# A fourth pair of converted-weight buffers in the expert loop, and one transposition a unit earlier

## What is computed

```
def expert(args):
    wg, wu, wd, ix, g = args
    xe = t[ix]
    he = jax.nn.silu(xe @ wg) * (xe @ wu)
    return (he @ wd) * g[:, None].astype(he.dtype)
```

## Time and profile before

| | us |
|---|---|
| median of 3 runs | 2207.47 |
| lowest, highest run | 2193.83, 2209.68 |
| profiled execution, device time | 2186.04 |
| its span, first to last instruction | 2184.2 |
| PE busy | 2122.7 (97%) |
| DVE busy | 1570.7 (72%) |
| ACT busy | 1359.3 (62%) |
| mean DMA rate over the span | 286 GB/s |

### The profile page before, as it was taken

How to read it: one execution, slowest core, us unless ns; L and a number is a source line. 1 busy time by engine, 2 the same in 40 slices (tenths; PEclk the granted TensorE clock), 3 DMA queues, 4 the chain that set the end, 5 groups by cost and what they waited for, 6 DMA issues and landing times.

```text
span 2184.2 us, 27119 instructions
## 1 busy us (share of the span) xinstructions
PE 2122.7 (97%) x10388; PEld 1580.5 (72%) x10388; DVE 1570.7 (72%) x1203; ACT 1359.3 (62%) x1069; POOL 232.9 (11%) x138
## 2 busy tenths in 40 slices
PE   8999999999959999999999999999999999999997
PEld 6858878887846776777677777767767777777765
DVE  5384452234458887888888888888888888798885
ACT  5273362223226777777777777777777777767764
POOL 2102210000120101010110101001010101101010
PEclk9999999999979999999999999999999999999998
DMA  6202131132328999999999999999999999999994
GB/s 235 77 18 105 55 122 58 61 132 71 152 104 325 368 388 363 379 370 377 375 369 377 375 380 371 367 384 366 376 372 381 372 370 388 366 374 375 375 367 184
DMA packets 71916, 623.96 MB, mean 286 GB/s; under 512 B 8352, under 2 KB 8480, under 8 KB 19264
## 3 DMA queue, kind: packets, MB, share of 16 engines
q1 hardware_dynamic: 64128, 595.70, 70.5%
q0 software_dynamic: 7744, 27.67, 4.4%
HBM read 609.70 MB, written 13.63 MB: 285 GB/s over the span
## 4 chain that ended last, share of the span: by engine, by line
PE 84%; DVE 6%; DMA 6%; ACT 3%; issue 1%; POOL 0%; SPq 0%; ACTq 0%; DVEq 0%; POOLq 0%
PE PS L543 26%; PE PS L545 25%; PE PS L544 25%; DMA x_w_raw<-in_w_expert_gate 4%; DVE x_w_low L1187 3%; ACT x_w_high L1117 2%; PE PS L652 2%; PE PS L898 1%; PE PS L635 1%; DMA x_w_raw<-in_w_expert_up 1%; PE PS L666 1%; PE PS L552 1%; DMA w_raw<-in_w_in 1%; PE PS L842 1%; PE PS L763 0%
## 5 line engine op out<-in xcount | busy, mean ns | idle before, releaser
L1187 DVE TENSOR_TENSOR x_w_low<-x_w_raw,x_w_high 128x3072 fp32r<-128x3072 f32 x383 | 1177.9, 3087 | 234.2 <-ACT x_w_high L1117 232.1
L1117 ACT ACTIVATE x_w_high<-x_w_raw 128x3072 fp32r<-128x3072 f32 (+1 forms) x384 | 980.3, 2558 | 259.7 <-PE PS L545 197.7
L543 PE MATMUL PS<-x_w_high,xT_high 128*96 128x512 f32 (+1 forms) x1536 | 580.0, 378 | 4.9 <-DVE x_w_low L1187 4.8
L545 PE MATMUL PS<-x_w_high,xT_low 128*96 128x512 f32 (+1 forms) x1536 | 575.1, 374 | 0.0
L544 PE MATMUL PS<-x_w_low,xT_high 128*96 128x512 f32 (+1 forms) x1536 | 573.2, 373 | 0.0
L543 PEld LDWEIGHTS PS<-x_w_high,xT_high 128*96 128x96 f32 x1536 | 248.1, 162 | 98.8 <-DVE x_w_low L1187 13.3
L545 PEld LDWEIGHTS PS<-x_w_high,xT_low 128*96 128x96 f32 x1536 | 248.0, 161 | 90.1
L544 PEld LDWEIGHTS PS<-x_w_low,xT_high 128*96 128x96 f32 x1536 | 248.6, 162 | 85.7
L543 PE MATMUL PS<-x_w_high,hidden_high 128*96 128x512 f32 x704 | 281.2, 399 | 0.0
L545 PE MATMUL PS<-x_w_high,hidden_low 128*96 128x512 f32 x704 | 276.6, 393 | 0.0
L544 PE MATMUL PS<-x_w_low,hidden_high 128*96 128x512 f32 x704 | 275.8, 392 | 0.0
(11 more groups left out here) (189 smaller groups left out, 1703.3 us busy)
## 6 DMA issues: line engine op xcount, KB each, us to landing
x_w_raw<-in_w_expert_gate SPq DMA_DIRECT2D x96, 1536.0 KB, 8.5
x_w_raw<-in_w_expert_up SPq DMA_DIRECT2D x96, 1536.0 KB, 8.8
x_w_raw<-in_w_expert_down SPq DMA_DIRECT2D x96, 1536.0 KB, 8.5
x_w_raw<-in_w_expert_gate SPq DMA_DIRECT2D x32, 1024.0 KB, 7.3
x_w_raw<-in_w_expert_up SPq DMA_DIRECT2D x32, 1024.0 KB, 7.3
x_w_raw<-in_w_expert_down SPq DMA_DIRECT2D x32, 1024.0 KB, 7.1
w_raw<-in_w_in SPq DMA_DIRECT2D x19, 1024.0 KB, 4.8
x<-in_x_sample SPq DMA_DIRECT2D x8, 512.0 KB, 11.5
```

Source lines behind the costliest of these rows:

```text
L543: mm(out, sh, mh, start=first, stop=False)
L545: return mm(out, sl, mh, start=False, stop=last)
L1117: a_(xh[:, w % SPLITS, 0:n], xraw[:, w % RAWS, 0:n], ACT.Copy).then_inc(x_high, 1)
L1187: return v.tensor_tensor(out, src, high.bitcast(F32), ALU.subtract)
```

## The change

`SPLITS` goes from 3 to 4. The four pairs are no longer one array with an index but four arrays each; the fourth pair lies at columns 960 and 4032, where the residual rows were. ACT therefore converts unit 3 ahead of the loop too, behind the first two halves of tokens and behind a wait for all six residual stores, and DVE makes its low part before the loop. In the loop, step u converts unit u + 4. `tokens` 1 goes from behind unit 22 to behind unit 21, after `hidden` 5: with four pairs, the low part that stands behind `tokens` 1 in step 22 is that of unit 2 of the next expert, and in step 21 that of unit 1, which is the first that reads the second half of the tokens.

```diff
@@ -88,7 +88,7 @@
-RAWS, SPLITS = 4, 3
+RAWS, SPLITS = 4, 4
@@ -101,7 +101,7 @@
         after("up", 2, 1): [("tokens", 0)], after("down", 1, 1): [("hidden", 4)],
-        after("down", 1, 2): [("hidden", 5)], after("down", 2, 0): [("tokens", 1)]}
+        after("down", 1, 2): [("hidden", 5), ("tokens", 1)]}
@@ -194,14 +194,14 @@
-        xl = at("x_w_low", 7104, SPLITS * XUNIT, dt=F32R).rearrange("p (b n) -> p b n", b=SPLITS)
-        xh = at("x_w_high", 16320, SPLITS * XUNIT, dt=F32R).rearrange("p (b n) -> p b n", b=SPLITS)
+        xl = [at(f"x_w_low{i}", off, XUNIT, dt=F32R) for i, off in enumerate((7104, 10176, 13248, 960))]
+        xh = [at(f"x_w_high{i}", off, XUNIT, dt=F32R) for i, off in enumerate((16320, 19392, 22464, 4032))]
...
-        xraw = at("x_w_raw", 31680, RAWS * XUNIT).rearrange("p (b n) -> p b n", b=RAWS)
+        xraw = [at(f"x_w_raw{i}", off, XUNIT) for i, off in enumerate((31680, 34752, 37824, 40896))]
...
@@ -1114,13 +1114,13 @@
                 n = unit_width(w)
-                a_(xh[:, w % SPLITS, 0:n], xraw[:, w % RAWS, 0:n], ACT.Copy).then_inc(x_high, 1)
+                a_(xh[w % SPLITS][:, 0:n], xraw[w % RAWS][:, 0:n], ACT.Copy).then_inc(x_high, 1)
...
-            for w in range(1, SPLITS):
+            for w in range(1, 3):
                 unit_high(0, w)
@@ -1136,6 +1136,8 @@
             for q in range(PRE):
                 misc_high("tokens", q, q + 1, 6 + q)
+            act.wait_ge(S("x", "residual_stored"), 16 * NT)
+            unit_high(0, 3)
...
@@ -1562,6 +1564,7 @@
             v.tensor_copy(idxi[:, 2:E + 1], idxf[:, 2:E + 1]).then_inc(S("rt", "tables"), 1)
             unit_low(0, 2)
+            unit_low(0, 3)
```

More of the change, by code:

```diff
@@ L402, in _ @@
                     b = w % RAWS
-                    sp.dma_start(xraw[:, b, 0:unit_width(w)], unit_source(e, w)).then_inc(x_loaded[b], 16)
+                    sp.dma_start(xraw[b][:, 0:unit_width(w)], unit_source(e, w)).then_inc(x_loaded[b], 16)
         @block.gpsimd
@@ L495, in _ @@
             pool.wait_ge(x_high, 1)
-            nc.gpsimd.tensor_tensor(xl[:, 0, 0:n], xraw[:, 0, 0:n], xh[:, 0, 0:n].bitcast(F32), ALU.subtract
+            nc.gpsimd.tensor_tensor(xl[0][:, 0:n], xraw[0][:, 0:n], xh[0][:, 0:n].bitcast(F32), ALU.subtract
                                     ).then_inc(x_split, 1)
@@ L862, in _ @@
                         f0, nf = DT[q][c]
-                        uh, ul = (a[:, b, 0:nf * D].rearrange("p (f d) -> p f d", f=nf) for a in (xh, xl))
+                        uh, ul = (a[b][:, 0:nf * D].rearrange("p (f d) -> p f d", f=nf) for a in (xh, xl))
                         last_round = [r for r, (r0, rn) in enumerate(HR[q]) if r0 < f0 + nf][-1]
@@ L875, in _ @@
                         k0, nk = KT[q][c]
-                        uh, ul = (a[:, b, 0:unit_width(w)].rearrange("p (k f) -> p k f", k=nk) for a in (xh, xl))
+                        uh, ul = (a[b][:, 0:unit_width(w)].rearrange("p (k f) -> p k f", k=nk) for a in (xh, xl))
                         if kind == "gate" and c == 0 and q > 0:
@@ L1544, in unit_low @@
                 dve.wait_ge(x_high, e * NXU + w + 1)
-                low(xl[:, w % SPLITS, 0:n], xraw[:, w % RAWS, 0:n], xh[:, w % SPLITS, 0:n]).then_inc(x_split, 1)
+                low(xl[w % SPLITS][:, 0:n], xraw[w % RAWS][:, 0:n], xh[w % SPLITS][:, 0:n]).then_inc(x_split, 1)
             def misc_low(what, j, n, n_high, bank):
```

## The result

The changed kernel took 2193.22 us (median of 20 runs, 2175.14 to 2195.35), the kernel before on the same chip 2191.78 us (20 runs, 2186.05 to 2209.68). The ratio is 0.9942, with a 95% interval from 0.9916 to 0.9967: faster by 0.6%, inside the 1% that the prediction called the same. The forecast was 2198.

A forecast was written before the change was run, and what follows sets the result against it. PE was taken to set the pace, with the DMA engines close to full. From the median 2207.5 us, 7.4 for PE's waits gave 2200, and about 2 more gave 2198; own range 2190 to 2206, all cases 2177 to 2212.

The forecast's parts named there:

- the 1% that the prediction called the same: Whole kernel: about 1% (22 us) is what a measurement tells from no change; chance of the same 0.74.
- its mechanism: Expert loop: each conversion carries the next unit, giving PE reserves of 3.6 and 2.8 us, so all 15 waits vanish.
- the start lies in idle time: Ahead of the loop: unit 3's conversion and low part fit in idle time of ACT and DVE; gain 0.
- the transposition keeps 0.7 us: Behind unit 21: `hidden` 4 is read before the `tokens` 1 transposition with a reserve of 0.6 us; cost 0.
- All in front of unit 3 or unit 7: Expert loop: all 15 late starts of PE stand before these two units, losing 7.4 us together.
- The term -7.4: Expert loop: the fourth pair removes PE's 15 late starts, a gain of 7.4 us from the measured distances.
- The first rival: Expert loop: the timed runs hold more such waits, all removed; 2178.7 us, a gain of 1.3%; chance 0.20.
- The 21.4 us between the profiled execution and the timed runs: Timed median over profiled execution; the trace can't show what fills it; a tenth, about 2 us, counted as gain.
- the other rival: Expert loop: DMA engines bound the timed runs, 389 GB/s at most; gain 0 to 3 us, 2204 to 2207; chance 0.21.
- the clock times of the conversions stay: Expert loop: trigger and raw ring unchanged, so conversions keep their times and each carries the next unit.
- the gather as hidden: Expert loop: POOL's gather for the expert after next starts one unit (4.2 us) earlier, at no cost.
- ACT's waits turning to the loads: Expert loop: a sign the prediction is wrong, if ACT's waits turn from PE to loads and DMA share rises to 1.

The follow-up runs named there:

- the second profile of the kernel before: The kernel before, no edit, run once more with a profile: 2191.87 us, span 2190.1; late starts of PE sum to 13.7 us in 26 places.
- the six raw buffers: Changed kernel with six raw buffers and three pairs instead of four and four, transposition still moved: 0.9912 of the kernel before, 2176.7 us at the high clock.
- the pair alone: Changed kernel with the `tokens` 1 transposition back behind unit 22, fourth pair and separate arrays kept: 0.9964 of the kernel before, 2175.8 us at the high clock.
- the doubled low part: DVE makes the low part of unit 4 twice per expert: 1.0013 in the changed kernel, 0.994 with the transposition back behind unit 22, both against the kernel before.
- three raw buffers with the pair alone: Changed kernel with three raw buffers instead of four and the `tokens` 1 transposition back behind unit 22: 1.1324 of the kernel before.
- the move alone: Changed kernel with three pairs instead of four, so only the moved transposition and separate arrays remain: 1.0035 of the kernel before, 2198.8 us at the high clock.
- the arrays alone: The kernel before with separate arrays for the buffers, three pairs and the transposition unmoved: 1.0036 of the kernel before.

## Why the prediction was right

*The forecast and its mechanism held.* No distance over 0.35 us is left in front of any unit, the waits for low parts are gone, the DMA share is 0.96 to 0.98 between 750 and 2080 us, the expert period is 93.94 us, the start lies in idle time, the transposition keeps 0.7 us. The undoing experiments give the cause: without the pair there is no gain, and with nothing but the pair there is all of it.

*What was luck.* That the median came within 5 us of 2198. The changed kernel has no run between 2178.3 and 2193.2, and 11 of 20 were at the low clock; with nine there its median would have been near 2178, at the lower end of the range. The 2198 stands on a median of 2207.47 from three runs, two of them at the low clock; over 20 runs the median before is 2191.78, and the two medians by themselves show no gain.

*The places.* "All in front of unit 3 or unit 7" is a wrong reading: unit 3 in 2 of 15 places, unit 4 in 5, unit 7 in 8. The chain of expert 2 showed the exception. Its load of unit 3 took 9.10 us, the longest of 14, whose median is 6.8; the load of unit 4 takes 10.4. The argument survives, since it holds for any unit: what is late for one unit is in time for the next.

*The term -7.4.* In the profiled pair it is 7.8. At equal clock over all runs it is 12.8 to 14.1. The term was sized on one execution that had few waits; the second profile of the kernel before had 13.7 us of them. The first rival (more waits in the timed runs) was right to that extent, by some 6 us and not by 21.4.

*The 21.4 us between the profiled execution and the timed runs.* The prediction left them open, with two rivals that explained them by the loop. Neither was the main cause. The medians jump with the number of runs that have the mean clock of 0.982. Of the profiled executions of kernels that run dry little or never, two had it (the six raw buffers, and the pair alone with the doubled low part), and both show the same place, near 305 us and long before the experts, in a part that the change does not touch. PE's wait for the window of values (us, times, longest) with six raw buffers, and then in the changed kernel's profile:

```profile
PE PS L654 <- DMA v_windows<-v_dram: 2.4, 1, 2.4
```

```profile
PE PS L652 <- DMA v_windows<-v_dram: 0.7, 1, 0.7
```

The table of stretches of the kernel with six raw buffers, PE alone (us; busy; granted clock; DMA share; GB/s):

```profile
300.00:310.00 10.00, 7.64 (x55) 0.94 0.66 207
310.00:320.00 10.00, 10.00 (x43) 0.50 0.10 39
320.00:330.00 10.00, 10.00 (x42) 0.50 0.01 2
330.00:340.00 10.00, 10.00 (x43) 0.50 0.00 1
340.00:350.00 10.00, 10.00 (x56) 0.86 0.14 33
```

and the same 50 us as one stretch in the kernel with the pair alone and the doubled low part (wait 1.7 us) and in the changed one:

```profile
300.00:350.00 50.00, 48.31 (x227) 0.62 0.17 53
```

```profile
300.00:350.00 50.00, 49.31 (x327) 1.00 0.23 77
```

A wait of 2.4 or 1.7 us at 305 us is followed by some 35 us at a granted clock of 0.50, that is 1.2 instead of 2.4 GHz. Some 35 us of work at half speed are 17 us lost, the distance of the two groups. A third profile, of three raw buffers with the pair alone, has 2.6 us there and the same fall. In the other eleven the wait is absent or up to 1.3 us, and the clock stays at 1.00. The loop's stretches have a clock of 1.00 in both of the first two, which answers what was asked with the second profile of the kernel before: the two groups do not part in the loop. So of the 21.4 us about 18 are this clock and some 3.5 the loop's own variation (2186.04 against the 2189 that such runs take). For the timed runs, which have no trace, it is inferred from their mean clock alone, and what makes the transfer late in some executions is open. The bound on the DMA engines that the other rival needed (389 GB/s at a share of 1) did not appear: the stretches of the changed kernel between 750 and 2080 us carry 374 to 379 GB/s with PE fully busy, and its gain is the same in both groups of runs. The Trainium skill's 425 GB/s (DMA: Bandwidth & Descriptors, section Measured) would have ruled that rival out as well; no run here shows that rate, since PE asks for no more than 379.

*The step that did not hold: "the clock times of the conversions stay".* One load of each expert is issued 6.75 us behind the start of unit 21 in all these kernels (of unit 3 with three pairs, of unit 4 with four, both of up and 1.5 MB), and what is issued at this moment lands later now. For one expert, in the kernel before, with the move alone, with the pair alone, and after:

```profile
DMA to landing us min/median/max: 6.8/6.8/6.8
```

```profile
DMA to landing us min/median/max: 9.7/9.7/9.7
```

```profile
DMA to landing us min/median/max: 9.0/9.0/9.0
```

```profile
DMA to landing us min/median/max: 10.5/10.5/10.5
```

Over 14 experts the medians are 6.8, 8.4, 8.8 and 10.5 us (the expert shown for the move alone is one of its longer ones). One half goes with the move, in both pairs of kernels that differ by it (8.4 against 6.9 with the arrays alone, 10.5 against 8.8). POOL's gather used to be issued 1.2 us behind that load, and with the move it is issued 2.9 us ahead of it. The gather of the kernel before, then of the changed one:

```profile
1221.61 3.18 POOL L505 DMA_INDIRECT gathered<-t_dram,idxi  x1 [78.15 <-PE PS L842]
```

```profile
1214.62 3.70 POOL L505 DMA_INDIRECT gathered<-t_dram,idxi  x1 [69.58 <-PE PS L842]
```

The prediction counted the gather as hidden because nobody waits for its tokens. But its transfer now runs ahead of this load of the ring. The next load tells the same story the other way round: the gather used to be issued 2.4 us ahead of it, and with the move is 7.0 us ahead. With three pairs it is that of unit 4, which took 10.6 us with the arrays alone and takes 8.3 with the move; with four it is that of unit 5 (1 MB), 9.7 and 8.9. In the kernel before the load just behind the gather is that of unit 4, a unit that PE waited for in 5 of 15 and in 11 of 26 places: the gather that nobody waits for may have been part of the loss from the start. But other loads take as long far from it (that of unit 6 10.2 us before and 10.3 after). That the gather, rather than the transposition's other effects, delays the load is the likely reading and was not tried by itself. It is also the likely source of the 8 us that the move adds with three pairs, and of most of the 2.6 against 15.5 us of the doubled low part. The other half, 6.8 to 8.8 with the pair alone, was not taken apart either; the pair shifts which sizes of load surround this one.

*The waits by name.* The prediction said that ACT's waits turning to the loads would show it wrong, together with a DMA share of 1. The first happened (66.7 instead of 29.4 us), and the share stayed at 0.96. Read alone, that sign would have misled: it shows that the loads are later, and the cover of a unit, 4.2 us, absorbs both.

## The best version

The changed kernel (2176.8 us at the high clock), the pair alone (2175.8) and the six raw buffers (2176.7) are within a microsecond, which these runs cannot order. The pair alone keeps a reserve of about 3.4 us in front of unit 4, against 1.7 to 3.1 in most experts of the changed kernel, so of the two I would keep it. None of the three has a wait of PE in the loop; what is left there is PE's own pace of 0.23 us per 512-column product. Left open is the 1 to 3 us of the separate arrays. The wait for the windows of values, worth some 17 us in four to five of ten runs, is the larger prize; shortening it was not tried.

## What to carry to other kernels

A buffer in a ring buys lateness, up to the work it holds, and no bandwidth: count the dry moments of the engine behind it, in two profiles rather than one, since here they differed by a factor of two. A transfer that nobody waits for is not free: here moving it one step ahead went with a slower load behind it and a faster one after that. Name the place where an engine runs dry by counting over the whole loop, and not from one expert: here that one was the exception. And before explaining a difference of 1% between runs by the stage you are working on, sort the runs by mean granted clock, and look where in the profile the clock fell, since waits in the loop can lower the mean as well.

## What was not expected of the hardware

- A single PE wait of 1.7 us or 2.4 us was followed by some 35 us at half the clock, while waits of up to 1.3 us at the same place, in eleven other profiles, left it at 1.00. In the loop PE's 2.6 us waits behind unit 21 were followed by some products at half speed in nine of 15 experts, less than one unit of them.
- An indirect gather issued ahead of a 1.5 MB load instead of behind it went with a landing 1.5 us later (8.4 against 6.9 us) with three pairs, and 1.8 us later (10.54 against 8.79) with four, while the next load landed 2.3 us (10.6 to 8.3) and 0.7 us (9.66 to 8.94) earlier.
- With three raw buffers the 16 DMA engines carried 312 GB/s at a share of 0.85, with four 377 at 0.96 to 0.97: 17% fewer bytes, but only 12% less busy time, so the share of busy time by itself understates the room.
